# Experts that work on 96 token slots at a time in place of 128, in a two-layer decoder trunk on one core

## The reference

```python
def moe_swiglu(h, w_router, w_gate, w_up, w_down):
    logits = (h @ w_router).astype(jnp.float32)
    top_vals, top_idx = lax.top_k(logits, TOP_K)          # TOP_K = 2 of N_EXPERTS = 8
    top_w = jax.nn.softmax(top_vals, axis=-1)
    gates = jnp.sum(jax.nn.one_hot(top_idx, N_EXPERTS, dtype=jnp.float32) * top_w[..., None], axis=-2)
    y = jnp.zeros_like(h)
    for e in range(N_EXPERTS):                            # w_gate, w_up: 1024 x 3584; w_down: 3584 x 1024
        y = y + gates[..., e:e + 1] * swiglu(h, w_gate[e], w_up[e], w_down[e])
    return y
```

## Time and profile before

| | |
|---|---|
| median of 3 runs | 1533.07 us (1532.9 to 1536.39) |
| the profiled execution | 1533.65 us, its span 1531.9 us |
| busy share of the span | PE 99%, PEld 83%, DVE 77%, ACT 61%, POOL 8% |
| granted clock | 0.997 of full speed on average |
| start of the experts' matmuls | about 567 us |

### The profile page before, as it was taken

The page is one execution under the profiler, slowest core; times in us unless marked ns, Lnnn a source line. Parts: engine busy times, 40 slices in busy tenths (PEclk is TensorE's granted clock), DMA queues, the critical chain, the costliest instruction groups (busy, mean ns, idle before and its releaser), DMA issues.

```text
span 1531.9 us, 21333 instructions
## 1 busy us (share of the span) xinstructions
PE 1515.5 (99%) x8472; PEld 1271.1 (83%) x8472; DVE 1174.2 (77%) x1081; ACT 929.1 (61%) x861; POOL 124.1 (8%) x90
## 2 busy tenths in 40 slices
PE   8999999999999999999999999999999999999998
PEld 6899989999975668888888888888888888888886
DVE  5987475444444569898898898898988988987985
ACT  3455445344423447677776777677777777777673
POOL 1481020000011000000000000000000000000000
PEclk9999999999999999999999999999999999999999
DMA  5413496455554259999999999999999999999990
GB/s 186 144 58 111 147 330 252 167 196 189 168 198 133 108 180 365 376 371 379 382 372 381 379 380 372 383 383 362 387 385 358 386 383 360 391 381 356 397 372 29
DMA packets 186689, 445.64 MB, mean 291 GB/s; under 512 B 5517, under 2 KB 5669, under 8 KB 186624
## 3 DMA queue, kind: packets, MB, share of 16 engines
q1 hardware_dynamic: 182528, 430.52, 76.3%
q0 software_dynamic: 4096, 14.20, 3.3%
HBM read 437.86 MB, written 7.89 MB: 291 GB/s over the span
## 4 chain that ended last, share of the span: by engine, by line
PE 94%; DVE 3%; ACT 1%; DMA 1%; issue 0%; SPq 0%; POOL 0%; DVEq 0%; ACTq 0%
PE bank L1363 13%; PE bank L1365 13%; PE bank L1364 13%; PE bank L1348 7%; PE bank L1350 7%; PE bank L1349 7%; PE bank L659 4%; PE bank L1035 3%; PE bank L1034 3%; PE bank L1033 3%; PE bank L1157 2%; PE bank L1074 2%; PE bank L1022 1%; PE bank L1021 1%; PE bank L1023 1%; PE bank L736 1%
## 5 line engine op out<-in xcount | busy, mean ns | idle before, releaser
L2351 DVE TENSOR_TENSOR ring_r<-ring,buf_r 128x2048 fp32r<-128x2048 f32 x336 | 751.4, 2285 | 31.4 <-ACT buf_r L1720 31.4
L1720 ACT ACTIVATE buf_r<-ring 128x2048 fp32r<-128x2048 f32 x336 | 629.3, 1914 | 52.1 <-PE bank L1350 43.1
L1363 PE MATMUL bank<-ring_r,buf_r 128*128 128x512 f32 x896 | 355.2, 396 | 0.2 <-DVE buf_r L2470 0.2
L1365 PE MATMUL bank<-buf_r,buf_r 128*128 128x512 f32 x896 | 349.7, 390 | 0.0
L1364 PE MATMUL bank<-buf_r,buf_r 128*128 128x512 f32 x896 | 349.0, 389 | 0.0
L1365 PEld LDWEIGHTS bank<-buf_r,buf_r 128*128 128x128 f32 x896 | 168.2, 188 | 36.2
L1364 PEld LDWEIGHTS bank<-buf_r,buf_r 128*128 128x128 f32 x896 | 168.5, 188 | 33.5
L1363 PEld LDWEIGHTS bank<-ring_r,buf_r 128*128 128x128 f32 x896 | 168.3, 188 | 33.3 <-DVE buf_r L2470 0.3
L1348 PE MATMUL bank<-ring_r,buf_r 128*128 128x512 f32 x440 | 172.8, 393 | 0.0
L1350 PE MATMUL bank<-buf_r,buf_r 128*128 128x512 f32 x440 | 171.5, 390 | 0.0
L1349 PE MATMUL bank<-buf_r,buf_r 128*128 128x512 f32 x440 | 171.2, 389 | 0.0
(11 more groups left out here) (347 smaller groups left out, 1886.1 us busy)
## 6 DMA issues: line engine op xcount, KB each, us to landing
ring<-in_moe_w_gate SPq DMA_DIRECT2D x56, 2048.0 KB, 8.8
ring<-in_moe_w_up SPq DMA_DIRECT2D x56, 2048.0 KB, 8.9
ring<-in_moe_w_down SPq DMA_DIRECT2D x56, 2048.0 KB, 9.1
ring<-in_a_w_in SPq DMA_DIRECT2D x8, 2048.0 KB, 8.4
ring<-in_dense_w_gate SPq DMA_DIRECT2D x7, 2048.0 KB, 9.2
ring<-in_dense_w_up SPq DMA_DIRECT2D x7, 2048.0 KB, 8.1
ring<-in_dense_w_down SPq DMA_DIRECT2D x7, 2048.0 KB, 7.9
ring<-in_a_w_out SPq DMA_DIRECT2D x2, 2048.0 KB, 11.0
```

The lines of the kernel that those rows point to most:

```text
L1363: pe.matmul(o, xh, low[:, c], start=k == 0, stop=False)
L1365: ins = pe.matmul(o, xh, high[:, c], start=False, stop=k == KT - 1)
L1720: act.activation(HB[m % NHB], half_words(m, U_MOE), ACT.Copy).then_inc(m_wh, 1)
L2351: dve.tensor_tensor(half_low(m, U_MOE), half_words(m, U_MOE), HB[m % NHB], ALU.subtract).then_inc(m_wl, 1)
```

## The change

`WIN` is 96 instead of 128. `NWIN` becomes 3 (two full windows and a part of a third cover 256 tokens) and `ITEMS` 24. Nothing else is edited; all tiles and slices that are cut by `WIN`, `NWIN` and `ITEMS` follow.

```diff
 EXPERTS = 8
-WIN = 128
+WIN = 96
 NWIN = -(-S // WIN)
 ITEMS = NWIN * EXPERTS
 SLOTS = 7
```

## The result

The kernel after took 1544.07 us (median of 4, 1542.42 to 1544.42) against 1532.99 us: a ratio of 1.0059, 95% interval 1.0042 to 1.0076. Eight more executions beside the experiments gave 1539.36 us against 1533.03 us, 1.0045 (1.0029 to 1.006). One execution of the kernel before, beside these, took 2175.28 us at a mean granted clock of 0.652 and is left out of that ratio. I had forecast 1523.5 us, with 1508 to 1532 as the range.

A forecast was written before the change was run, and what follows sets the result against it. The prediction took PE's instruction stream in the experts as the bound; transposes -7.6, index and gate products -1.6 and first token block -0.4 made -9.6 us, forecast 1523.5 us, range 1508 to 1532.

The forecast's parts named there:

- What bounds the kernel: Expert stage: PE's own instruction stream sets the item time, 119.6 us; transfers are paced by PE.
- The 4032 expert matmuls: Experts' fp32r matmuls: interval stays 226.7 ns with 96 stationary columns, 0 us; ends -49 and +327 us.
- D: Rival, expert matmuls: weight load of 96 columns no longer covered, 81 ns a matmul, about 1850 us; chance 0.07.
- Transposes: PE's transposes in the experts: streaming side sets their time, 109 to 82 ns each, -7.6 us in all.
- rival C: Transposes get no cheaper because the load of 128 columns sets them; 1531 us, chance 0.18.
- Index and gate products: Small fp32 products in `index` and `gather_pick`: shorter loads at 96 columns, -1.6 us in all.
- The first token block: `gather_rows` and the DVE, ACT, DVE chain behind it: tiles a quarter smaller, -0.36 us.
- work beside the path: DVE, ACT and POOL work in the experts off PE's path: savings count 0; `windows()` +0.3 us, covered.
- The sum: Whole kernel: -7.6 - 1.6 - 0.4 = -9.6 us, giving a forecast of 1523.5 us.
- rival A: Expert matmul interval follows the columns, 24 cycles instead of 32: -13.4 us more, 1510 us, chance 0.17.
- B: Rival: expert matmul interval falls to the fp32 pass, -49 us more, 1474 us; chance 0.05.
- The general path: Fallback whose bound falls from 128 to 96 tokens: not taken, busiest expert has 71; taken, it adds 1914 us.

The follow-up runs named there:

- slots128: Kernel before, with the expert matmuls using only 96 of the 128 columns of their stationary operand: 1545.66 us, ratio 1.0066.
- stride128: Kernel after, with token and hidden blocks 512 bytes apart again and 96 columns used as stationary operand: 1533.66 us, ratio 0.9998.
- stat128: Kernel after, with 96 token slots but 128 stationary columns in the expert matmuls and blocks 512 bytes apart: 1526.17 us, ratio 0.9952.
- cols64: Kernel before, with only 64 of the 128 stationary columns used in the expert matmuls (timing only, layer not computed): 1542.25 us, ratio 1.0069.

## Why the prediction was wrong, point by point

**What bounds the kernel** held: PE sets the item in every version, none of the fourteen traces shows a wait of PE between 700 and 1340 us, and transfers, DVE and ACT are behind it.

**The 4032 expert matmuls** is the step that failed: "I take the interval as unchanged: 0 us". It went from 226.7 to 231 ns. In the traces the time between fp32r matmuls grew by 1.63 us an item, 13 us in all, and this term stood at nothing in the sum. The reasoning was that a load already covered gains nothing by being shorter; I took the converse, that it can't lose either, from two rows with the same 128 columns. The range of that step ran from -49 to +327 us, but I gave its upper side 0.07 and priced it by a load whose 81 ns of growing part are all uncovered. What was measured is another mechanism than D's: the load records are shorter (161 ns, well below the interval), the load queue is idle more, not less, and the interval is longer still. In items: the column count is +1.19 us (slots128), 2.4 ns a matmul over the 504, or +1.01 us with 96 slots (stride128 less stat128); the distance of the blocks +0.68 us (after less stride128), 1.4 ns. What in the chip makes either stays open. The closing sentence of the prediction, that as little as 2 ns decides, was right, and so was the sign that the load record would be 161 ns.

On the rule of the Trainium skill ("TensorE: Matmul & The Clock Gate", section "Weight-path perf modes"), that the fast weight load needs just 128 columns: its sign is that of the runs, as a stationary operand short of 128 columns costs time. But load records of 188, 184, 174, 161, 134 and 109 ns lie on one line, and 124 columns lose 0.21 us an item where 112 lose 1.25. No fast load that ends below 128 is to be seen in them. So the runs don't bear out the rule's mechanism for fp32r, and I had dismissed its direction together with it.

**Transposes** held in the main: 82 to 83 ns from start to start where 109 were, and 63 ns with 72 columns, so the streaming side sets them and rival C falls. The group of four cost 0.33 us in the kernel after (0.34 forecast), but a part of that agreement is luck. Of the 36 transposes in an item only 28 are followed by another one. From the last of each group to the start of the next fp32r matmul it is 28 ns in both kernels, and the interval behind that is longer than the others: 315 ns before, and again 315 in stat128:

```profile
995.16 0.49 PE L663 MATMUL bank<-cst,xbuf 96*128 96x96 f32 x4
995.44 0.48 PE L1367 MATMUL bank<-ring_r,buf_r 128*128 128x512 f32 x1
995.75 0.39 PE L1368 MATMUL bank<-buf_r,buf_r 128*128 128x512 f32 x1
```

It is 287 ns only where both the transposes and the expert matmuls have the 96 of the change (stride128, and 286 in the kernel after), and still 316 in slots128:

```profile
993.24 0.45 PE L1367 MATMUL bank<-ring_r,buf_r 128*96 128x512 f32 x1
993.52 0.39 PE L1368 MATMUL bank<-buf_r,buf_r 128*96 128x512 f32 x1
```

So in stat128 the transposes gave 28 x 26 ns = 0.72 us an item of the 36 x 27 = 0.97 forecast. **Index and gate products** gave 0.16 us of 0.2. With 0.07 us in the other intervals these are the measured 0.95 of 1.17.

**The first token block** and the **work beside the path** were as forecast or too small to tell: DVE's tiles of 384 elements take 553 ns (552 to be expected), ACT's 513.

**The sum.** By the traces, an item of the kernel after less one of the kernel before is -0.72 us (between transposes), -0.16 us (index and gate products) and +1.63 us (between fp32r matmuls), +0.74 us before rounding. The single experiments, 1.19 (columns) + 0.68 (distance) - 0.95 (cheaper parts) = +0.92, overshoot by 0.18, which is the difference between the two prices of the column count, 1.19 and 1.01. It lies in the interval behind the transposes: 28 ns less in each of 8 groups, 0.2 us, only where both changes are there. Eight items make 6 us, and these are the 6 us between like executions. Rivals A and B (a shorter interval) fall: fewer columns never made it shorter. The general path was not taken.

**The range.** It left out the other side at 0.07. Of a step that multiplies by 4032, an unknown of 1% is 9 us, the whole forecast gain; the chance that it isn't zero had to be larger, and on both sides. That the first measurement lay 11 us above the kernel before, and not 6, is the chance of its start and no part of the mechanism. Two slips in the prediction change nothing: 1347.0 us is the last and not the first record of the index group of item 7 (0.04 us an item), and the range has 1508 for rival A, whose own sum gives 1510.

## What to carry to other kernels

Where one instruction form fills the engine that sets the time, a change of its shape has to be priced on the chip before the rest is summed: 3 to 4 ns on each of 4032 matmuls outweighed everything else that the edit saved. A stationary operand of 128 columns, padded with values that nobody reads, was faster here than any of 124 to 32 that does less; so cut the streaming operands (the transposes) and leave the stationary one full. If it has fewer columns, keep its blocks 512 bytes apart: of the three distances tried with 96 columns that was the best. And with effects of 0.5%, compare executions with a like start: four runs of one kernel all fell here in the group that is 4 to 5 us later.

## What the runs showed of the hardware

In these traces an fp32r matmul that streams 512 columns at 2.4 GHz is started every 226.7 ns with 128 stationary columns and every 230 ns on average with 112 to 64, though its weight load is shorter (174 to 134 ns against 188) and the load queue idles longer. The transposes and index products disturb the intervals just behind them; from the ninth on, 97% of those with 128 columns (before) are 226 or 227 ns, while with 64 they go through a pattern of 224 to 236 ns. In the trace of cols64 it is seen from 999.77 us on as 240, 230, 240, 220, 230, 220, 240, 230 and 240 ns, as far as two decimals show it:

```profile
999.77 0.40 PE L1368 MATMUL bank<-buf_r,buf_r 128*64 128x512 f32 x1
1000.01 0.39 PE L1369 MATMUL bank<-buf_r,buf_r 128*64 128x512 f32 x1
1000.24 0.40 PE L1367 MATMUL bank<-ring_r,buf_r 128*64 128x512 f32 x1
1000.48 0.39 PE L1368 MATMUL bank<-buf_r,buf_r 128*64 128x512 f32 x1
1000.70 0.39 PE L1369 MATMUL bank<-buf_r,buf_r 128*64 128x512 f32 x1
1000.93 0.39 PE L1367 MATMUL bank<-ring_r,buf_r 128*64 128x512 f32 x1
1001.15 0.40 PE L1368 MATMUL bank<-buf_r,buf_r 128*64 128x512 f32 x1
1001.39 0.39 PE L1369 MATMUL bank<-buf_r,buf_r 128*64 128x512 f32 x1
1001.62 0.40 PE L1367 MATMUL bank<-ring_r,buf_r 128*64 128x512 f32 x1
1001.86 0.39 PE L1368 MATMUL bank<-buf_r,buf_r 128*64 128x512 f32 x1
```

What makes the pattern (the timing of the load against the stream, or how the operand's addresses fall) no run here settles; only that it comes with the column count at unchanged addresses, and the mean gets worse with blocks 448 or 384 bytes apart (from the ninth interval on, 230.0 ns at 512 bytes, 230.9 at 448, 231.5 at 384, all with 96 columns). With 32 columns it is 231.7 ns.

The interval behind a group of transposes hangs on both sides of it: 315 ns (before), 315 (stat128) and 316 (slots128), but 286 to 287 where the transposes stream 96 columns and the stationary operand behind them has 96 too.
